# Gated tiles four ahead, the few tokens' rows in small pieces, weight units of both expert products in pairs of 1024 KB

## The chip, the cores and the metric

One core of a Trainium2 chip. The metric is the device time of one launch in microseconds. The kernel before takes 2781.53 us, the median of 3 runs (2779.76 to 2782.51).

## The reference

256 tokens of width 2048, everything in 32-bit floats, two blocks one after the other. The first has attention (16 forgetting heads, 16 dilated heads) and then a product-key expert layer, which is what the change is about:

```python
def peer(x, w_query, sub_keys, expert_down, expert_up):
    ...
    experts = (i1 * PEER_N_KEYS + i2).reshape(T, PEER_HEADS * PEER_TOPK)       # 128 of 16384 per token
    gates = jax.nn.softmax(top_vals, axis=-1).reshape(T, PEER_HEADS * PEER_TOPK).astype(x.dtype)
    ...
        u = jnp.take(expert_down, ec, axis=0)
        hdn = jax.nn.gelu(jnp.einsum('ted,td->te', u, xc))
        vsel = jnp.take(expert_up, ec, axis=0)
        return jnp.einsum('te,ted->td', gc * hdn, vsel)
```

The second block has a gated convolution, a chunked recurrence, an output product and a gated side input.

## The kernel before

**The expert layer is computed densely.** Instead of gathering 128 rows per token, the kernel multiplies 224 of the 256 tokens (`DENSE`) with all 16384 experts: the *down product* gives the hidden values of 128 experts per tile (`group_down`, 128 tiles), GELU is applied, each value is multiplied with its gate (zero for experts that weren't chosen; the gates are scattered into `gate_scratch` in HBM by 256 indirect DMAs of GpSimd and read back 8 tiles at a time by `load_g`), and the *up product* adds 128 gated tiles into eight PSUM banks. The last 32 tokens (`FEW`) are done the other way: GpSimd gathers 128 rows of 8 KB (1 MB) at a time, 32 times from `expert_down` and 32 times from `expert_up`, and VectorE multiplies and adds them (`few`, L1482 and L1487, one in about 1.4 tiles of the up product). What these tokens need (their expert numbers, gates, scale, their rows `x4` of the spilled activations, the gain row in `lent[0]`, the matrix `back`) is loaded by SyncE in the down product, at `FEW_LOADS`.

**Weights come as units** of [128, 1024] floats, 512 KB: two per tile in both products, 4 KB per partition. SyncE loads unit u into slot u % 4 of `raw` (`NRAW` = 4) when unit u - 4 has been split. ScalarE rounds it to whi (L1832, out whi, in raw), VectorE subtracts to get the remainder wlo (L1026), three units ahead of TensorE (`NSPL` = 3), and TensorE multiplies whi and wlo in turn (L590). Unit u may be split when TensorE has done unit u - 3. Each engine runs a list of steps that was written out by hand: `step(u)` ends with `split(u + 3)`, and whatever else an engine has to do stands before or behind it in a fixed order.

**A gated tile** of the up product is made by `weight(i)`: VectorE multiplies hidden values by gates (out HB, in HB and aX, L1029), ScalarE makes the rounded copy (L1832, out aX), VectorE subtracts (out aX, in HB and aX, L1029). For tile i + 2 this happens behind step 2i + 1 of the product, that is behind the split of the first unit of tile i + 2. TensorE waits for the gated tile (`s_ul`), for whi and for wlo. The copies stand in a ring of eight (`wring`).

**SyncE's list.** `now` = u - 6 while `load(u)` is the newest load. At `now == FEW_LOADS` 18 transfers are issued in a row. Gates are loaded every eighth tile (1 MB in rows of 1 KB), from the 64th tile on pieces of the spilled activations (256 KB). All are in the same queue as the weight units.

Of the kernel before, what the change touches and what calls it, by code (L numbers as in the profile page):

```python
# [147 lines left out]
def _build(nc, I, out, ctx):  # L148
# [135 lines left out]
    def lent_before(k):  # L284

        return [j for j in range(k) if lent_to(j) == lent_to(k)]

    FEW_AT = {(4 + 5 * k if k < 6 else 31 + 36 * (k - 6) // 25 if k < PICKS else 71 + 42 * (k - PICKS) // 31): k for k in range(2 * PICKS)}

    C = ExitStack()  # L290
# [32 lines left out]
    grow1 = HB[:, 8192:10240]  # L323
    C.close()

    plan = Plan(I)
    G = plan.groups
    for name, key in (("dv", "w_dv"), ("fv", "w_fv")):
# [34 lines left out]
    SCF = [plan.fill([b for b in range(4, 8) if b != R3F[0]][k % 3]) for k in range(8)]  # L363
    for i in range(128):
        plan.group("down", i, "w_down", i, 1, True)
    late = [G["down", 127].fills[0][0], G["down", 126].fills[0][0], R3F[0], SCF[-1][0]]
    early = [b for b in range(8) if b not in late]
    UPB = [early[0], early[1], late[0], late[1], early[2], early[3], late[2], late[3]]
# [2 lines left out]
    UPS = [(i, half) for i in range(120) for half in range(2)] + [(i, half) for half in range(2) for i in range(120, 128)]  # L371
    plan.src += [I["w_up"][i, :, half * UNIT:half * UNIT + UNIT] for i, half in UPS]
    UP1 = len(plan.src)
    for kp, b in enumerate((early[2], early[3], early[0], early[1], early[2], early[3], late[2], late[3])):
        plan.turn("mix", kp, plan.fill(b))
    plan.side_by_side("fl", "w_in2", range(40, 44), [plan.fill(b) for b in (early[0], early[1], late[0], late[1])])
# [30 lines left out]
    NU = len(plan.src)  # L407
    TURNED = plan.turned
    DOWN0 = G["down", 0].first
    FEW_LOADS = DOWN0 + 188  # L410
    down_rows, up_rows = I["down_rows"], I["w_up"].rearrange("i p d -> (i p) d")
    SQ0 = 6
    ROWS0 = G["dv", 1].first + 4
# [62 lines left out]
    def _(e):  # L476
        w = Gate(e)

        def load(u):
            if u >= NU:  # L480
                return
            if u >= NRAW:
                w.wait_ge(s_lo, u - NRAW + 1)
            e.dma_start(raw[:, u % NRAW, 0:plan.src[u].shape[-1]], plan.src[u]).then_inc(s_raw[u % NRAW], 16)

        def load_g(n, a=0, z=8):
            i = n % 2
# [8 lines left out]
        for u in range(NRAW, NU + NRAW + NSPL):  # L496
            load(u)
            if u == 6:
                e.dma_start(small[:, :], I["small"][:, 0:256]).then_inc(s_const, 16)
                e.dma_start(X[:, 0, :], I["x"][:, 0:D]).then_inc(s_x[0], 16)  # L500
            if u == 8:
                e.dma_start(X[:, 1, :], I["x"][:, D:2 * D]).then_inc(s_x[1], 16)
            if u == 11:
                e.dma_start(attc[:, :], I["att"]).then_inc(s_att, 16)
                e.dma_start(fbr[:, :], I["forget_bias"]).then_inc(s_att, 16)
            now = u - NRAW - NSPL + 1
            if now == G["fg", 0].end + 1:

                w.wait_ge(s_fc, 2)
                e.dma_start(c_d, cT[:, :]).then_inc(s_cd, 16)  # L510
                w.wait_ge(s_cd, 16)
                e.dma_start(CB[:, :, :].rearrange("p h c -> p (h c)"),
                            c_d.rearrange("h c -> (h c)").unsqueeze(0).to_broadcast([128, 4096])).then_inc(s_cb, 16)
            if now == PQ0 + 2:
                for i in range(2, 4):
                    for b, n in G["wf", i].fills:
                        w.wait_ge(s_free[b], n)
                e.dma_start(h1_d, X[:, :, :].rearrange("p t d -> p (t d)")).then_inc(s_spill, 16)
            if now == PQ0 + 5:

                for kp in range(8):
                    (b, n), q = TURNED["ffn", kp]
                    w.wait_ge(s_free[b], n)
                    w.wait_ge(s_nt, q + 1)
                w.wait_ge(s_spill, 16)
                e.dma_start(hb(5120, 2048), I["keys"]).then_inc(s_keys, 16)
            if now in ZERO:
                z = ZERO.index(now)
                w.wait_ge(s_zs, 1)
                e.dma_start(g_z[:, z * 2048:z * 2048 + 2048], zeros).then_inc(s_zf, 16)  # L530
            if now == FEW_LOADS:
# [6 lines left out]
                last = slice(128 - FEW, 128)  # L538
                for j in range(SHARE):
                    to, of = slice(FEW * j, FEW * j + FEW), slice(PICKS * j, PICKS * j + PICKS)  # L540
                    e.dma_start(eid4[to, :], eid[last, of]).then_inc(s_few, 16)
                    e.dma_start(gate4[to, :], gate[last, 1, of]).then_inc(s_few, 16)
                    e.dma_start(r4[to, :], st[last, 25:26]).then_inc(s_few, 16)
# [12 lines left out]
            if UP0 < now <= UP1 and (now - UP0) % 2 == 0:  # L556
                i = (now - UP0) // 2 - 1
                if i == 64:
                    w.wait_ge(s_uh, 66)
                    w.wait_ge(s_ul, 66)  # L560
                if i >= 64 and i % 4 == 0 and i < 96:
                    n = (i - 64) // 4
                    e.dma_start(HB[:, n * 512:n * 512 + 512], h1_d[:, n * 512:n * 512 + 512]).then_inc(s_h1r, 16)
                if i == 96:
                    e.dma_start(grow1, I["final_norm_gain"].to_broadcast([128, D])).then_inc(s_row1, 16)
            if now == G["fl", 0].first:

# [18 lines left out]
    def _(e):  # L586
# [125 lines left out]
        def tick(u):  # L712
# [11 lines left out]
            if u == ROWS3 + 4:  # L724
                row_of(R3F, 2, ones, diag)
            if u == UP1 - 16:
                w.wait_ge(s_few, 64 * SHARE + 32)
# [284 lines left out]
    def _(e):  # L1012
# [7 lines left out]

        def split(u):
            if u < NU:
                n, r, s = plan.src[u].shape[-1], u % NRAW, u % NSPL
                w.wait_ge(s_raw[r], 16 * (u // NRAW + 1))
# [567 lines left out]
        for i in range(120):  # L1592
# [4 lines left out]
                w.wait_ge(s_fg2, 1)  # L1597
                tt(hid4[:, :], hid4[:, :], gate4[:, :], ALU.mult).then_inc(s_fv, 1)
            step(UP0 + 2 * i + 1)
            weight(i + 2 + (i > 116))  # L1600
            if i == 116:
                weight(119)
            lower_bounds(i)
            if i == 90:
                tt(cols[:, C_NMX:C_NMX + 16], cols[:, C_NMX:C_NMX + 16], cols[:, C_FIN:C_FIN + 16], ALU.mult).then_inc(s_gm, 1)
        for j in range(16):
            step(UP0 + 240 + j)
            if j < 5:
                weight(123 + j)

        for j in range(2):
            for i in range(4):
# [129 lines left out]
    def _(e):  # L1742
# [39 lines left out]
        w.wait_ge(s_few, 64 * SHARE + 32)  # L1782
# [39 lines left out]
    def _(e):  # L1822
# [14 lines left out]

        def split(u):
            if u < NU:
                n, r, s = plan.src[u].shape[-1], u % NRAW, u % NSPL  # L1840
                w.wait_ge(s_raw[r], 16 * (u // NRAW + 1))
# [204 lines left out]
        for kt in range(16):  # L2046
            w.wait_ge(s_xt[XT_OF[kt]], 16)
            act(aX[:, kt, 0:256], xT[:, kt, :], ACT.Copy, scale=cols[:, C_ATT + kt:C_ATT + kt + 1]).then_inc(s_xh, 1)
            if kt in (1, 3):
                u = kt // 2  # L2050
                w.wait_ge(s_raw[u], 16)
                act(whi[:, u, 0:512], raw[:, u, 0:512], ACT.Copy).then_inc(s_h0, 1)
                act(whi[:, u, 512:1024], raw[:, u, 512:1024], ACT.Copy).then_inc(s_hi, 1)
            if kt in (7, 11):
                split((kt + 1) // 4)
        for name in ("dv", "fv"):
# [80 lines left out]
        for i in range(120):  # L2137
            step(UP0 + 2 * i)
            step(UP0 + 2 * i + 1)
            weight(i + 2 + (i > 116))  # L2140
            if i == 116:
                weight(119)
            if i == 68:
                w.wait_ge(s_fd2, PICKS)
                act(hid4[:, :], hid4[:, :], ACT.Gelu_apprx_tanh, scale=r4[:, 0:1]).then_inc(s_fg2, 1)
# [8 lines left out]
                warm()  # L2154
        for j in range(16):
            step(UP0 + 240 + j)
            if j < 5:
                weight(123 + j)

        for j in range(2):  # L2160
            for i in range(4):
# [104 lines left out]
def arrays(inp):  # L2266
# [11 lines left out]
    def toks(w):  # L2278
# [12 lines left out]
    a["w_out"] = toks(g["w_out"][0])  # L2291
    a["w_pq"] = feat(g["peer_query"][0])
    a["w_down"] = np.ascontiguousarray(
        g["peer_down"][0].reshape(128, 128, 2, 8, 128).transpose(0, 2, 4, 3, 1)).reshape(128, 2, 128, 1024)
# [34 lines left out]
```

## Time and profile before

| | |
|---|---|
| median of 3 runs | 2781.53 us (2779.76 to 2782.51) |
| the profiled execution | 2780.66 us, span of the core 2778.8 us |
| TensorE busy | 2731.4 us (98%) |
| VectorE, ScalarE, GpSimd busy | 1941.7, 1399.1, 794.8 us |
| mean granted clock of TensorE | 0.997 |
| moved by DMA | 628.32 MB, mean 226 GB/s |
| down product | about 496 to 1158 us |
| up product | about 1160 to 1895 us |

The span is one execution from its first to its last instruction; the time of that execution is 1.9 us longer. Engines work side by side, so busy shares don't add up to the span; what a wait costs is read from the engine that the others wait for. A line such as L1029 is that of a helper, so the tiles' names (out <- in) tell what an instruction does.

### The profile page before, as it was taken

To read this page: it belongs to the slowest core of one execution; us is meant where nothing else is said; L and a number is where in the kernel's file an instruction comes from. 1 tells how busy PE (TensorE), PEld (TensorE's weight loads), DVE (VectorE), ACT (ScalarE), POOL (GpSimd) and SP (SyncE) were. 2 spreads that over 40 slices of the span, in tenths; PEclk is the share of its full clock that TensorE was granted. 3 is DMA by queue.
4 is the path that set the end of the run, shared out by engine and by line. 5 is a ranking of instruction groups with operands and counts; after the bars stand their busy time and mean duration, and the time that the engine had idled before them with its cause. 6 is when DMAs were issued, how large, how long until landed. Compare 5 with 4: busy or idle time off the path is not lost.

```text
span 2778.8 us, 39198 instructions
## 1 busy us (share of the span) xinstructions
PE 2731.4 (98%) x14906; PEld 2369.9 (85%) x14906; DVE 1941.7 (70%) x2979; ACT 1399.1 (50%) x2003; POOL 794.8 (29%) x477
## 2 busy tenths in 40 slices
PE   9999999999999999999999999999999999999998
PEld 7887888999999989988777777778888888999886
DVE  6567666888888656666778788766778876555555
ACT  5455654555555545544444434446755545444454
POOL 0012200388888888400111121201201111000000
PEclk9999999999999999999999999999999999999999
DMA  7654478888888788777899999865655556666664
GB/s 275 209 166 134 147 254 301 277 209 209 210 209 209 209 212 208 235 249 267 314 335 326 323 339 352 321 219 185 190 179 153 162 157 193 189 189 188 187 199 157
DMA packets 205195, 628.32 MB, mean 226 GB/s; under 512 B 50944, under 2 KB 67600, under 8 KB 193616
## 3 DMA queue, kind: packets, MB, share of 16 engines
q1 hardware_dynamic: 162800, 558.24, 63.3%
q0 software_dynamic: 42064, 67.51, 8.8%
q8 instruction: 119, 1.95, 0.3%
q14 instruction: 68, 0.56, 0.1%
q10 hardware_dynamic: 144, 0.07, 0.0%
HBM read 604.59 MB, written 21.10 MB: 225 GB/s over the span
## 4 chain that ended last, share of the span: by engine, by line
PE 80%; DVE 8%; issue 4%; ACT 4%; DMA 3%; SPq 0%; DVEq 0%; POOL 0%; ACTq 0%
PE bank L590 80%; DVE wlo L1026 5%; ACT whi L1832 3%; DMA raw<-in_w_up 2%; PE bank L602 1%; DVE HB L1487 1%; DVE HB L1029 1%; DVE HB L1482 1%; DMA HB<-in_down_rows,eid 0%; ACT aX L1832 0%; DMA aX<-gate_scratch 0%; DMA raw<-in_w_down 0%; DMA VV<-in_xT 0%; ACT L1832 0%; DVE aX L1029 0%
## 5 line engine op out<-in xcount | busy, mean ns | idle before, releaser
L1026 DVE TENSOR_TENSOR wlo<-raw,whi 128x1024 fp32r<-128x1024 f32 (+1 forms) x965 | 1195.6, 1241 | 716.0 <-ACT whi L1832 712.1
L1832 ACT ACTIVATE whi<-raw 128x1024 fp32r<-128x1024 f32 (+1 forms) x967 | 1013.7, 1054 | 891.7 <-PE bank L590 840.1
L590 PE MATMUL bank<-whi,aX 128*128 128x512 f32 x2944 | 922.7, 392 | 25.5 <-DVE aX L1029 23.9
L590 PE MATMUL bank<-aX,whi 128*128 128x448 f32 (+2 forms) x4000 | 920.1, 379 | 0.0
L590 PEld LDWEIGHTS bank<-aX,whi 128*128 128x128 f32 (+1 forms) x4000 | 728.6, 188 | 98.7 <-issue 3.7
L590 PEld LDWEIGHTS bank<-whi,aX 128*128 128x128 f32 x2944 | 552.4, 188 | 159.9 <-DVE aX L1029 40.6
L590 PE MATMUL bank<-wlo,aX 128*128 128x512 f32 x1472 | 572.0, 390 | 1.4 <-DVE wlo L1026 1.4
L1777 POOL DMA_INDIRECT gate_scratch<-gate,place x256 | 529.3, 2067 | 77.9 <-issue 77.6
L590 PE MATMUL bank<-aX,wlo 128*128 128x224 f32 (+2 forms) x3984 | 513.5, 279 | 7.2 <-DVE wlo L1026 7.0
L590 PEld LDWEIGHTS bank<-aX,wlo 128*128 128x128 f32 (+1 forms) x3984 | 499.6, 191 | 22.8 <-DVE wlo L1026 8.0
L590 PEld LDWEIGHTS bank<-wlo,aX 128*128 128x128 f32 x1472 | 276.4, 188 | 58.4 <-DVE wlo L1026 2.5
L1832 ACT ACTIVATE aX<-HB 128x224 fp32r<-128x224 f32 x128 | 49.9, 391 | 316.6 <-DVE HB L1029 316.6
L1812 POOL TENSOR_TENSOR tmpc<-tmpc,rows 128x256 f32<-128x256 f32 x64 | 58.0, 906 | 405.8 <-DVE tmpc L1029 405.8
L1795 POOL DMA_INDIRECT HB<-in_down_rows,eid x32 | 50.7, 1586 | 335.7 <-DVE hid L1482 330.1
L1795 POOL DMA_INDIRECT HB<-in_w_up,eid x32 | 53.1, 1660 | 221.5 <-DVE HB L1487 177.5
L1750 POOL TENSOR_TENSOR EB<-EB,dn 128x256 f32<-128x256 f32 (+1 forms) x32 | 31.1, 992 | 276.6 <-DVE dn L1110 225.7
L1029 DVE TENSOR_TENSOR aX<-HB,aX 128x224 fp32r<-128x224 f32 x128 | 50.1, 392 | 57.6 <-ACT aX L1832 57.6
L1482 DVE CUSTOM_DVE_ANT_0 HB<-HB 128x2048 f32<-128x2048 f32 x32 | 73.1, 2284 | 0.7 <-DMA HB<-in_down_rows,eid 0.7
L1487 DVE SCALAR_TENSOR_TENSOR HB<-HB,hid 128x2048 f32<-128x2048 f32 x31 | 72.7, 2346 | 0.0
L1832 ACT ACT_TABLE_LOAD x52 | 66.7, 1283 | 2.5 <-PEq L2320 1.2
L1818 POOL TENSOR_TENSOR X<-X,grow 128x512 f32<-128x512 f32 x6 | 9.5, 1578 | 179.0 <-ACT scr L1832 179.0
L1029 DVE TENSOR_TENSOR HB<-bank,HB 128x224 f32<-128x224 f32 (+1 forms) x144 | 55.6, 386 | 3.7 <-ACT HB L1832 3.7
(246 smaller groups left out, 2066.6 us busy)
## 6 DMA issues: line engine op xcount, KB each, us to landing
raw<-in_w_down SPq DMA_DIRECT2D x256, 512.0 KB, 4.4
raw<-in_w_up SPq DMA_DIRECT2D x256, 512.0 KB, 5.4
raw<-in_w_in SPq DMA_DIRECT2D x176, 512.0 KB, 3.7
raw<-in_w_out SPq DMA_DIRECT2D x32, 512.0 KB, 4.2
gate_scratch<-HB SPq DMA_DIRECT2D x16, 1024.0 KB, 7.5
raw<-in_w_pq SPq DMA_DIRECT2D x32, 512.0 KB, 5.6
raw<-in_w_o SPq DMA_DIRECT2D x32, 512.0 KB, 4.1
raw<-in_w_pg SPq DMA_DIRECT2D x32, 512.0 KB, 3.7
```

What stands on the lines that cost most here:

```text
L590: return e.matmul(o, lhsT, rhs, start=start, stop=stop, skip_group_check=True)
L602: return e.transpose(o, src, ident)
L1026: e.tensor_tensor(wlo[:, s, 0:n], raw[:, r, 0:n], whi[:, s, 0:n].bitcast(F32), ALU.subtract).then_inc(s_lo, 1)
L1029: return e.tensor_tensor(o, a, b, op)
L1482: e.tensor_tensor_reduce(lent[n], lent[n], x4, 1.0, 0.0, ALU.mult, ALU.add, hid4[:, k:k + 1]).then_inc(s_fd2, 1)
L1487: e.scalar_tensor_tensor(acc4, lent[n], hid4[:, j:j + 1], acc4, ALU.mult, ALU.add).then_inc(s_fv, 1)
L1750: last = e.tensor_tensor(p, p, d2[:, :, k:k + 1].to_broadcast([128, 2, c.stop - c.start]), ALU.mult)
L1777: e.indirect_dma_start(g_d, bass.IndirectOffsetOnAxis(ap=place[0:some, t, n:n + 1], axis=0), gate[0:some, t, n:n + 1], None, compute_op=AL ...
L1795: e.indirect_dma_start(lent[n], None, up_rows if k >= PICKS else down_rows, bass.IndirectOffsetOnAxis(ap=eid4[:, k % PICKS:k % PICKS + 1], ...
L1812: e.tensor_tensor(h, h, rows4[:, :], ALU.mult).then_inc(s_rw, 1)
L1818: e.tensor_tensor(X2[:, t, f], X2[:, t, f], grow2[:, f], ALU.mult).then_inc(s_gg, 1)
L1832: return e.activation(o, i, f, **k)
```

## The change

Three things. **(1)** The up product's gated tiles are made up to four tiles ahead instead of two (`TILES_AT`; the lead is built up in the first six tiles, two of whose steps make two). **(2)** The transfers for the few tokens begin eight units earlier, at unit 180 of the down product; twelve small ones and `back` are issued in a row, the four pieces of `x4` (256 KB each) and the gain row in four pieces of 256 KB (rows of 2 KB) follow one by one, every third unit. **(3)** The two units of a tile of the down product, and of the first 120 tiles of the up product, are loaded by one transfer of 1024 KB into two neighbouring slots, 8 KB per partition (for that the down weights are laid out in HBM with both halves in a row). It is issued when unit u - 3 has been split, instead of u - 4, and both units wait for the same semaphore. `SLOT` shifts the slots by three so that pairs are neighbours.

```diff
+    TILES_AT, n = {}, 2
+    for i in range(120):
+        z = min(i + 3 + (i >= 2) + (i >= 5), 128)
+        TILES_AT[i] = range(n, z)
+        n = z
...
+    WIDE = {G["down", i].first: rows_down[i].rearrange("p (u c) -> p u c", u=2) for i in range(128)}
...
+    WIDE |= {UP0 + 2 * i: I["w_up"][i].rearrange("p (u c) -> p u c", u=2) for i in range(120)}
...
-    FEW_LOADS = DOWN0 + 188
+    SLOT = [(u + 3) % NRAW for u in range(NU)]
+    LANDED, landings = {}, [0] * NRAW
+    for u in range(NU):
+        if u - 1 in WIDE:
+            LANDED[u] = LANDED[u - 1]
+        else:
+            landings[SLOT[u]] += 16
+            LANDED[u] = s_raw[SLOT[u]], landings[SLOT[u]]
+    FEW_LOADS = DOWN0 + 180
+    X4_LOADS, GAIN_LOADS = [FEW_LOADS + 6 + 6 * j for j in range(SHARE)], [FEW_LOADS + 9 + 6 * j for j in range(4)]
...
         def load(u):
-            if u >= NU:
+            if u >= NU or u - 1 in WIDE:
+                return
+            r = SLOT[u]
+            if u in WIDE:
+                w.wait_ge(s_lo, u - NRAW + 2)
+                e.dma_start(raw[:, r:r + 2, :], WIDE[u]).then_inc(LANDED[u][0], 16)
                 return
             if u >= NRAW:
                 w.wait_ge(s_lo, u - NRAW + 1)
-            e.dma_start(raw[:, u % NRAW, 0:plan.src[u].shape[-1]], plan.src[u]).then_inc(s_raw[u % NRAW], 16)
+            e.dma_start(raw[:, r, 0:plan.src[u].shape[-1]], plan.src[u]).then_inc(LANDED[u][0], 16)
...
                     e.dma_start(r4[to, :], st[LAST, 25:26]).then_inc(s_few, 16)
-                    e.dma_start(x4[to, :], h1_d[last, D:2 * D]).then_inc(s_few, 16)
                 e.dma_start(back[:, :], I["small"][:, 256:384]).then_inc(s_few, 16)
-                e.dma_start(lent[0], I["ffn_norm_gain"].to_broadcast([128, D])).then_inc(s_few, 16)
+            if now in X4_LOADS:
+                j = X4_LOADS.index(now)
+                e.dma_start(x4[FEW * j:FEW * j + FEW, :], h1_d[LAST, D:2 * D]).then_inc(s_few, 16)
+            if now in GAIN_LOADS:
+                f = slice(GAIN_LOADS.index(now) * 512, GAIN_LOADS.index(now) * 512 + 512)
+                e.dma_start(lent[0][:, f], I["ffn_norm_gain"][:, f].to_broadcast([128, 512])).then_inc(s_few, 16)
...
             step(UP0 + 2 * i + 1)
-            weight(i + 2 + (i > 116))
-            if i == 116:
-                weight(119)
+            for x in TILES_AT[i]:
+                weight(x)
```

## Rows read from the trace of the kernel before

**Rows 1.** The page's first part: busy us, share, instructions of each engine.

```profile
PE 2731.4 (98%) x14906; PEld 2369.9 (85%) x14906; DVE 1941.7 (70%) x2979; ACT 1399.1 (50%) x2003; POOL 794.8 (29%) x477
```

**Rows 2.** Stretches: length, then busy PE, PEld, DVE, ACT, POOL; clock, DMA share, GB/s.

```profile
850.00:1000.00 150.00, 150.00 (x949) 142.29 (x949) 103.90 (x185) 81.60 (x123) 131.58 (x61) 1.00 0.80 207
1000.00:1020.00 20.00, 13.23 (x66) 12.22 (x65) 6.63 (x9) 5.47 (x9) 16.86 (x10) 0.74 0.91 261
1180.00:1350.00 170.00, 169.15 (x747) 139.72 (x746) 112.24 (x138) 74.46 (x93) 11.64 (x8) 1.00 0.76 262
1350.00:1830.00 480.00, 456.19 (x1959) 364.15 (x1958) 376.62 (x421) 199.41 (x255) 90.69 (x57) 1.00 0.92 331
```

**Rows 3.** Timeline of DVE, light part of the up product: start us, us, instruction, [idle before].

```profile
1244.61 1.22 DVE L1026 TENSOR_TENSOR wlo<-raw,whi 128x1024 fp32r<-128x1024 f32 x1 [1.21 <-ACT whi L1832]
...
1246.59 0.39 DVE L1029 TENSOR_TENSOR aX<-HB,aX 128x224 fp32r<-128x224 f32 x1 [0.46 <-ACT aX L1832]
1247.61 1.23 DVE L1026 TENSOR_TENSOR wlo<-raw,whi 128x1024 fp32r<-128x1024 f32 x1 [0.62 <-ACT whi L1832]
...
1252.03 0.39 DVE L1029 TENSOR_TENSOR aX<-HB,aX 128x224 fp32r<-128x224 f32 x1 [0.46 <-ACT aX L1832]
```

**Rows 4.** Waits in 1350 to 1830: who for whom, us in total, times, longest.

```profile
DVE wlo L1026 <- ACT whi L1832: 64.8, 85, 2.3
...
DVE aX L1029 <- ACT aX L1832: 37.5, 82, 0.5
...
PE bank L590 <- DVE aX L1029: 23.0, 36, 1.5
```

**Rows 5.** Timeline of DVE, crowded part: the subtractions that end three gated tiles.

```profile
1636.72 0.39 DVE L1029 TENSOR_TENSOR aX<-HB,aX 128x224 fp32r<-128x224 f32 x1 [0.46 <-ACT aX L1832]
...
1643.12 0.39 DVE L1029 TENSOR_TENSOR aX<-HB,aX 128x224 fp32r<-128x224 f32 x1 [0.46 <-ACT aX L1832]
...
1647.25 0.39 DVE L1029 TENSOR_TENSOR aX<-HB,aX 128x224 fp32r<-128x224 f32 x1 [0.46 <-ACT aX L1832]
```

**Rows 6.** Timeline of SyncE's queue and of ACT around the few tokens' transfers.

```profile
993.97 0.51 SPq L541 DMA_DIRECT2D eid<-eid  x1
...
995.79 0.58 SPq L544 DMA_DIRECT2D HB<-h_scratch  x1
...
1002.23 18.53 SPq L484 DMA_DIRECT2D raw<-in_w_down  x8
...
1010.43 1.06 ACT L1832 ACTIVATE whi<-raw 128x1024 fp32r<-128x1024 f32 x1 [10.20 <-DMA raw<-in_w_down]
```

**Rows 7.** Stretches of 2 us there, columns as in rows 2.

```profile
1006.00:1008.00 2.00, 0.10 (x1) 0.00 (x0) 0.00 (x0) 0.00 (x0) 1.69 (x2) 1.00 1.00 307
...
1012.00:1014.00 2.00, 1.14 (x5) 1.14 (x6) 2.00 (x3) 2.00 (x4) 1.95 (x1) 0.50 0.72 140
```

**Rows 8.** DMA issues, median us to landing: 520-990; 1180-1350 (two); 1350-1830 (two); 1250-1260.

```profile
raw<-in_w_down SPq DMA_DIRECT2D x186, 512.0 KB, 4.4
...
raw<-in_w_up SPq DMA_DIRECT2D x61, 512.0 KB, 4.7
...
HB<-in_down_rows,eid POOLq DMA_INDIRECT x8, 8.1
...
raw<-in_w_up SPq DMA_DIRECT2D x164, 512.0 KB, 5.9
...
HB<-in_w_up,eid POOLq DMA_INDIRECT x32, 8.7
...
raw<-in_w_up SPq DMA_DIRECT2D x3, 512.0 KB, 7.8
```

**Rows 9.** DMA issues of the whole run; then stretches, as rows 2, outside the products.

```profile
grow<-in_final_norm_g SPq DMA_DIRECT2D x1, 1024.0 KB, 5.8
...
2404.00:2406.50 2.50, 2.50 (x14) 2.09 (x14) 1.52 (x2) 1.52 (x3) 0.00 (x0) 1.00 0.68 210
...
2650.25:2653.50 3.25, 3.25 (x15) 2.65 (x15) 2.29 (x2) 2.22 (x3) 0.00 (x0) 1.00 1.03 416
```

More of the change, by code:

```diff
@@ L324, in _build @@
     C.close()
+    rows_down = I["w_down"]
+    I["w_down"] = rows_down.rearrange("i p (u c) -> i u p c", u=2)
     plan = Plan(I)
@@ L409, in _build @@
     DOWN0 = G["down", 0].first
-    FEW_LOADS = DOWN0 + 188
+    SLOT = [(u + 3) % NRAW for u in range(NU)]
[8 more added lines that the diff above has]
+    X4_LOADS, GAIN_LOADS = [FEW_LOADS + 6 + 6 * j for j in range(SHARE)], [FEW_LOADS + 9 + 6 * j for j in range(4)]
+    LAST = slice(128 - FEW, 128)
     down_rows, up_rows = I["down_rows"], I["w_up"].rearrange("i p d -> (i p) d")
@@ L537, in _ @@
                 w.wait_ge(s_spill, 16)
-                last = slice(128 - FEW, 128)
                 for j in range(SHARE):
                     to, of = slice(FEW * j, FEW * j + FEW), slice(PICKS * j, PICKS * j + PICKS)
-                    e.dma_start(eid4[to, :], eid[last, of]).then_inc(s_few, 16)
-                    e.dma_start(gate4[to, :], gate[last, 1, of]).then_inc(s_few, 16)
-                    e.dma_start(r4[to, :], st[last, 25:26]).then_inc(s_few, 16)
-                    e.dma_start(x4[to, :], h1_d[last, D:2 * D]).then_inc(s_few, 16)
+                    e.dma_start(eid4[to, :], eid[LAST, of]).then_inc(s_few, 16)
+                    e.dma_start(gate4[to, :], gate[LAST, 1, of]).then_inc(s_few, 16)
+                    e.dma_start(r4[to, :], st[LAST, 25:26]).then_inc(s_few, 16)
                 e.dma_start(back[:, :], I["small"][:, 256:384]).then_inc(s_few, 16)
-                e.dma_start(lent[0], I["ffn_norm_gain"].to_broadcast([128, D])).then_inc(s_few, 16)
+            if now in X4_LOADS:
[4 more added lines that the diff above has]
+                e.dma_start(lent[0][:, f], I["ffn_norm_gain"][:, f].to_broadcast([128, 512])).then_inc(s_few, 16)
             if now == UP0:
@@ L726, in tick @@
             if u == UP1 - 16:
-                w.wait_ge(s_few, 64 * SHARE + 32)
+                w.wait_ge(s_few, 64 * SHARE + 80)
                 w.wait_ge(s_fv, PICKS + 1)
@@ L1022, in split @@
             if u < NU:
-                n, r, s = plan.src[u].shape[-1], u % NRAW, u % NSPL
-                w.wait_ge(s_raw[r], 16 * (u // NRAW + 1))
+                n, r, s = plan.src[u].shape[-1], SLOT[u], u % NSPL
+                w.wait_ge(*LANDED[u])
                 w.wait_ge(s_hi, u + 1)
@@ L1607, in _ @@
             step(UP0 + 240 + j)
-            if j < 5:
-                weight(123 + j)
+            if j < 4:
+                weight(124 + j)
         for j in range(2):
@@ L1781, in _ @@
         e.dma_start(g0[:, :, :], g_v[:, 0:2, :]).then_inc(s_g0, 16)
-        w.wait_ge(s_few, 64 * SHARE + 32)
+        w.wait_ge(s_few, 64 * SHARE + 80)
         e.tensor_tensor(x4, x4, lent[0], ALU.mult).then_inc(s_fx, 1)
@@ L1839, in split @@
             if u < NU:
-                n, r, s = plan.src[u].shape[-1], u % NRAW, u % NSPL
-                w.wait_ge(s_raw[r], 16 * (u // NRAW + 1))
+                n, r, s = plan.src[u].shape[-1], SLOT[u], u % NSPL
+                w.wait_ge(*LANDED[u])
                 if u >= NSPL:
@@ L2050, in _ @@
                 u = kt // 2
-                w.wait_ge(s_raw[u], 16)
-                act(whi[:, u, 0:512], raw[:, u, 0:512], ACT.Copy).then_inc(s_h0, 1)
-                act(whi[:, u, 512:1024], raw[:, u, 512:1024], ACT.Copy).then_inc(s_hi, 1)
+                w.wait_ge(*LANDED[u])
+                act(whi[:, u, 0:512], raw[:, SLOT[u], 0:512], ACT.Copy).then_inc(s_h0, 1)
+                act(whi[:, u, 512:1024], raw[:, SLOT[u], 512:1024], ACT.Copy).then_inc(s_hi, 1)
             if kt in (7, 11):
@@ L2139, in _ @@
             step(UP0 + 2 * i + 1)
-            weight(i + 2 + (i > 116))
-            if i == 116:
-                weight(119)
+            for x in TILES_AT[i]:
+                weight(x)
             if i == 68:
@@ L2156, in _ @@
             step(UP0 + 240 + j)
-            if j < 5:
-                weight(123 + j)
+            if j < 4:
+                weight(124 + j)
         for j in range(2):
@@ L2293, in arrays @@
     a["w_down"] = np.ascontiguousarray(
-        g["peer_down"][0].reshape(128, 128, 2, 8, 128).transpose(0, 2, 4, 3, 1)).reshape(128, 2, 128, 1024)
+        g["peer_down"][0].reshape(128, 128, 2, 8, 128).transpose(0, 4, 2, 3, 1)).reshape(128, 128, 2048)
     a["down_rows"] = np.ascontiguousarray(g["peer_down"][0])
```

## Prediction

> **What bounds the kernel now.** The page first [rows 1]: TensorE is busy 2731.4 of 2778.8 us so at first sight nothing but TensorE counts. The stretches [rows 2] say where that is untrue: 6.8 us without a matmul in 1000 to 1020, at a mean clock of 0.74, and 23.8 us in 1350 to 1830; in 850 to 1000 nothing, in 1180 to 1350 0.9 us, both at full clock. The second stretch hides more than its idle time. Undisturbed, a tile of the up product (two weight units) takes 5.44 us from one gated tile to the next (1246.59 to 1252.03) [rows 3]; in 1350 to 1830 there are 82 gated tiles, at 5.44 us 446 us, and they took 480. So the loss there is 34 us.
>
> Who sets that pace? In 1350 to 1830 VectorE is busy 376.6 us and waits for ScalarE 64.8 + 37.5 us [rows 4]: sum 478.9 of 480, so VectorE never has to wait for TensorE. One tile in its order [rows 5]: remainder wlo of the even unit, gate times hidden (L1497's helper), wait 0.46 for ScalarE's rounded copy, subtraction, wait 0.62 for ScalarE's whi of the odd unit (queued behind that copy), remainder of the odd unit. From 1643.12 to 1647.25 that is 4.13 us; where a step of the few tokens' product (2.35 us) falls in, 1636.72 to 1643.12, 6.40 us. The two unavoidable waits are 1.08 x 82 = 88.6 us; busy plus these is 465.2, which is 19 us above TensorE's 446. The rest, 102.3 - 88.6 = 13.7 us, is late data: ScalarE splits late because its unit has not landed.
>
> The first stretch is one event [rows 6]. SyncE issues 18 transfers for the few tokens from 993.97 on and can issue the next unit's load only at 1002.23, 8.3 us later; that load shares the engines with 2 MB of rows and gains and lands at 1010.4, ScalarE having waited 10.20 us. TensorE is busy for 0.10 us of 1006 to 1008 and 1.14 us of 1012 to 1014, nothing between, and its clock, 1.00 as it stopped, is 0.50 (1.2 GHz of 2.4) when it resumes [rows 7]. By matmuls: 1000 to 1020 holds 66 where 850 to 1000 has 949 in 150 us [rows 2], that is 127 for 20 us; 61 x 0.158 us = 9.6 us.
>
> **The change part by part.** (1) *Small pieces.* SyncE now holds its queue for 13 issues: four groups of three and `back`. A group of three is 1.82 us (993.97 to 995.79) [rows 6], `back` about 0.5, so about 7.8 us, hardly less than before. But it begins right behind the load of a pair, and the next pair is due 5.02 us (a tile of the down product) later, so the delay is 2.8 us, and no 1 or 2 MB burst meets the load. The eight pieces of 256 KB follow every third unit (0.6 us of SyncE each, hidden). By the budget in (3) a pair may be some 2.5 us late before TensorE stands, so I leave 0.3 us and take 9.3 of the 9.6 us back; between 6 and 9.6.
>
> (2) *Tiles four ahead.* TensorE no longer waits for the gated tile (23.0 us of its waits in 1350 to 1830 end with VectorE's subtraction [rows 4]), but only for the remainder of its own unit, which VectorE finishes one um, copy and subtraction sooner: 1.2 us [rows 5]. VectorE's instructions, their order within a tile and both waits are the same, and it is VectorE that sets the pace in that stretch. So the 23.0 us are renamed, not removed: a once-only lead of 1.2 us. I take -1.2; between 0 and -5 (if it also smooths some of the late data).
>
> (3) *Pairs.* 512 loads of 512 KB become 248 of 1024 KB and 16 single ones. SyncE's issue time is no matter. What changes is how much lateness the loads may have. Before, unit u is requested when unit u-4 is split; now the pair (u, u+1) when u-3 is split, and the next-but-one request hangs on the split of u+1. That is a ring (the pairs of even and of odd number have one each, interleaved): request, landing L, whi 1.06 [rows 6], 0.1, wlo 1.22, then 3.0 us until the remainder of the odd unit is done (1245.83 to 1248.84 [rows 3]): L + 5.4 us for two tiles. TensorE's two tiles take 10.88 us, so the ring holds pace up to L = 5.45 us in the up product. Before, the ring was L + 2.4 for the same two tiles, with room to 8.4 us. In the down product the odd remainder follows the even one without the ScalarE round trip: L + 4.0 to 4.5 (one add, up to half a us of top-k work) for 10.04 us, so room to 5.6 to 6.0. Late by some 2.3 to 2.6 us once, TensorE isn't touched; late again and again, the ring sets the pace.
>
> What is L of a pair? No row has such a load. From below: a single load takes 4.4 us in the down product, 4.7 in the light part of the up product, 5.9 in the crowded part [rows 8]. A second 512 KB adds at least its bytes at the rate of the best stretch, 416 GB/s, 1.26 us [rows 9]; from the shape of a lone transfer (2.5 us at 210 GB/s, most of it ramp) about 1.0. From above: the only 1 MB load with 8 KB rows beside single loads there, `grow`, took 5.8 us behind a 512 KB one [rows 9]; and 2 x the 2.3 us a lone transfer lasts there gives +2.3. I take +1.1: down 5.5, light up 5.8. In the crowded part the engines are at 92% and 331 GB/s [rows 2]; there singles go from 4.7 to 5.9 while the 8 KB rows of the gathers only go from 8.1 to 8.7 [rows 8], so the long rows seem to get the larger share; with rows of 8 KB the pair should get a fairer one. I take 6.3 there (6.0 to 7.5).
>
> The Trainium skill (DMA: Bandwidth & Descriptors, Queues, rings and completion order) says that each engine goes round its queues packet by packet, which agrees with these landings; and the same page (Bandwidth) has the rule "Batch DMAs to ≥1 MiB for ≥75% of peak", which speaks for the pairs. By that page's fit for GpSimd's queue, 2.0 us + bytes/436e3, an estimate for 1 MB is 4.4 us, inside the room of 5.45, and the pairs would cost nothing.
>
> Price, up product. Light part, 30 tiles: (5.8 + 5.4) - 10.88 = 0.3 per two tiles, 5 us; each of four gate loads (1 MB ahead in the same queue; singles around the one at 1251.7 take 7.8 us [rows 8]) adds about 1 us that nothing gives back: 7 to 9, I take 8. Crowded part, 82 tiles: ring 6.3 + 5.4 = 11.7 against the 480/41 = 11.7 that it takes now: equal, but the ten gate loads now have no room: 1 to 1.5 us each, I take 12. Behind it nothing (no gathers, half the traffic). Down product: 5.5 against 5.6 to 6.0, 1 us for everything (0 to 8). Sum of pairs +21; from 0 (L = 4.4 to 5.0) to +55 (L one us longer: 0.5 us x 112 tiles more). Below zero too: with fairer shares the 13.7 us of late data may go.
>
> **Sum.** Profiled execution: 2780.66 us, of which the span is 2778.8. -9.3 - 1.2 + 21 = +10.5: 2791. The median of the runs is 0.9 us above the profiled one: I say 2792.
>
> **The rivals.** *A, pairs land in time* (faster). L of a pair is 5.0 or less. Then the ring costs nothing, the hiccup's 9.3 us and the 1.2 are won and some of the 13.7: 2781.5 - 10.5 - 8 = 2763. For it: rate 416 GB/s once a transfer runs, and that engines at 59% leave gaps; against it: 4.7 us for a single even in the light part. (The Trainium skill's batching rule, cited above, would give this case.) *A2, the idle time goes*: the tiles ahead remove the 23.8 us as the waits name them: 2781.5 - 9.3 - 24 = 2748. Against it: VectorE's full 478.9 us. *B, it balances*: pairs cost 5 to 14 us and the hiccup's return pays for it: 2781 ± 5. *C, the ring everywhere* (slower by more): L is 7 us or above in the crowded part and 6.5 in the down product; from L = 6.0 on the down product pays too, 256 units / 4 x 0.5 = 32 us, the up product 35 to 45: 2830.
>
> **Chances.** Forecast (2787 to 2810) 0.42; B 0.20; A 0.24; A2 0.05; C 0.09. A measurement of this kernel tells about 0.2%, 5.6 us, from no change: faster 0.29, same 0.20, slower 0.51. Signs are mixed, so beside the likeliest case's own 2787 to 2810 the range reaches from A's middle to the gap before C: 2760 to 2816.
>
> **What the profile after would show.** Landing of the 1024 KB loads: 5.5 / 5.8 / 6.3 us in the down, light and crowded parts; at 5.0 the forecast is wrong on the fast side. 1000 to 1020 with full clock and at most 1 us idle. TensorE's waits for the gated tile gone, and in their place waits for wlo; in 1180 to 1350 new idle of 5 to 10 us where there is 0.9 now. ScalarE's waits for the DMA of w_up stand at even units only, and are 40 us or more in all. VectorE's tile still 4.13 and 6.40 us where data is there. The forecast is wrong if the crowded part takes under 478 us, or if the down product's matmuls per us stay at 6.33 and the light part's at 4.39, for then the ring never closes.

## The result, and the profile after

The changed kernel takes 2803.43 us (median of 4 runs, 2801.33 to 2805.46), the kernel before, beside it, 2780.65 us (2778.54 to 2782.51): ratio 1.008, 95% interval 1.0065 to 1.0095. It is slower by 22.8 us. 2792 was forecast, range 2760 to 2816, slower with a chance of 0.51. The profiled execution is the slowest of the four (2805.46 us); its span is 2803.7 us, 24.9 more than before, and what is read from the two traces below adds up to that.

First the stretches of the changed kernel, columns as in [rows 2]:

```profile
1000.00:1020.00 20.00, 20.00 (x128) 18.97 (x128) 12.65 (x17) 11.56 (x20) 16.90 (x11) 1.00 0.93 265
...
1160.00:1180.00 20.00, 16.50 (x82) 13.64 (x80) 8.42 (x13) 8.68 (x14) 0.00 (x0) 0.97 0.61 212
1180.00:1350.00 170.00, 166.39 (x713) 134.40 (x714) 108.11 (x137) 71.97 (x92) 10.36 (x7) 0.98 0.69 244
1350.00:1850.00 500.00, 471.73 (x1970) 360.75 (x1969) 380.00 (x421) 199.94 (x255) 87.15 (x57) 1.00 0.87 320
```

The hole at 1000 us is gone: 128 matmuls at full clock where [rows 2] had 66. Against that, 1180 to 1350 holds 713 matmuls (747 before) with 3.6 us without a matmul (0.9 before), and the crowded part makes 1970 in 500 us, 3.94 per us; [rows 2] has 1959 in 480, 4.08. Two milestones divide the 24.9 us. VectorE's last scaling of a down tile (out HB, in HB and bank) starts 5.2 us sooner than before:

```profile
1173.34 0.39 DVE L1029 TENSOR_TENSOR HB<-HB,bank 128x224 f32<-128x224 f32 x1
```

in the timeline of VectorE before, and after

```profile
1168.16 0.39 DVE L1056 TENSOR_TENSOR HB<-HB,bank 128x224 f32<-128x224 f32 x1
```

TensorE's first transpose behind the up product comes 24.5 us later:

```profile
1894.97 0.60 PE L602 MATMUL bank<-small,X 128*128 128x128 f32 x4
```

in the timeline of TensorE before, and after

```profile
1919.44 0.60 PE L629 MATMUL bank<-small,X 128*128 128x128 f32 x4
```

So the up product took 29.7 us more, all before it 5.2 us less, and what lies behind it 0.4 us more (24.9 - 24.5).

Inside the up product the loss is placed by VectorE's timelines, by the start of the remainder (wlo) of the same unit in both traces (us; units of the up product counted from 0):

| unit | before | changed | changed later by |
|---|---|---|---|
| 0 | 1166.74 | 1161.55 | -5.2 |
| 8 | 1190.20 | 1190.45 | 0.3 |
| 64 | 1342.53 | 1348.71 | 6.2 |
| 240 | 1857.56 | 1882.04 | 24.5 |

The border of the two products cost 5.4 us, the light part 5.9, the crowded part 18.3, together the same 29.7. Now the waits of the changed kernel's whole run (who for whom: us in total, times, longest):

```profile
ACT whi L1858 <- DMA raw<-in_w_up: 134.1, 70, 5.3
ACT whi L1858 <- DMA raw<-in_w_down: 117.7, 56, 5.2
...
PE bank L617 <- DVE wlo L1053: 35.1, 58, 2.0
```

Before, the first two were 24.9 us (20 times) and 13.7 us (4 times). ScalarE now waits for nearly every second pair. TensorE's waits no longer name the gated tile (23.0 us in [rows 4]) but the remainder wlo. The 117.7 us in the down product hardly reach TensorE (2976 matmuls in 520 to 990, 2981 before), those in the up product do.

**The ring, seen once without and once with a gate load.** Timelines of VectorE, SyncE's queue and ScalarE in the changed kernel's light part, put in order of time (start us, us, instruction, [idle before]):

```profile
1211.14 1.23 DVE L1053 TENSOR_TENSOR wlo<-raw,whi 128x1024 fp32r<-128x1024 f32 x1 [0.56 <-ACT whi L1858]
...
1212.39 0.33 SPq L504 DMA_DIRECT2D raw<-in_w_up  x1
1212.77 0.43 SPq L514 DMA_DIRECT2D aX<-gate_scratch  x1
...
1216.83 0.33 SPq L504 DMA_DIRECT2D raw<-in_w_up  x1
...
1217.32 1.06 ACT L1858 ACTIVATE whi<-raw 128x1024 fp32r<-128x1024 f32 x1 [1.77 <-DMA raw<-in_w_up]
...
1218.48 1.23 DVE L1053 TENSOR_TENSOR wlo<-raw,whi 128x1024 fp32r<-128x1024 f32 x1 [1.68 <-ACT whi L1858]
...
1221.41 1.23 DVE L1053 TENSOR_TENSOR wlo<-raw,whi 128x1024 fp32r<-128x1024 f32 x1 [0.56 <-ACT whi L1858]
...
1224.04 1.06 ACT L1858 ACTIVATE whi<-raw 128x1024 fp32r<-128x1024 f32 x1 [2.66 <-DMA raw<-in_w_up]
```

An odd unit's remainder ends at 1212.37; SyncE requests the pair after the next at 1212.39; it lands at 1217.3, 4.9 us later; the even remainder follows at 1218.48 and the odd one ends at 1222.64. The ring was 10.27 us long, L + 5.4 as forecast, and under the 10.88 us of two tiles. The next pair was requested at 1216.83, behind the gate load of 1212.77, and took 7.2 us: its ring is 7.2 + 5.4 = 12.6, 1.7 us too long. (The page has no landing time for the 1024 KB loads; landings here are from SyncE's issue to the start of ScalarE's split where that waited for the transfer.) A landing can be read in this way only where ScalarE waited, so the early ones are missing. In the down product the mean of 56 such pairs was 5.5 us: the first six, beside the zeroing of the gate scratch, took 6.6 to 8.3 us, the 50 others 4.8 to 6.8, half of them at most 5.2. In the light part three pairs behind a gate load took 6.8 to 7.9 us and 14 others 4.7 to 7.3, nine of them at most 5.0. In the crowded part the mean of 51 pairs was 6.3 us, and 7.1 for the eleven of those just behind a gate load.

**The border of the two products**, which the forecast had not looked at. SyncE's queue and VectorE in the changed kernel:

```profile
1172.72 0.33 SPq L504 DMA_DIRECT2D raw<-in_w_up  x1
1173.17 0.97 SPq L514 DMA_DIRECT2D aX<-gate_scratch  x2
...
1180.10 0.39 DVE L1056 TENSOR_TENSOR HB<-HB,aX 128x224 f32<-128x224 f32 x1 [6.03 <-DMA aX<-gate_scratch]
```

and SyncE's queue before:

```profile
1173.04 0.33 SPq L484 DMA_DIRECT2D raw<-in_w_up  x1
1173.49 0.97 SPq L490 DMA_DIRECT2D aX<-gate_scratch  x2
```

The first gate loads are issued at the same moment in both, though the changed kernel was 5.2 us ahead. In SyncE's list they stand behind a weight load; as a pair it waits for one split more. VectorE stood 6.03 us for the gates; before it was 2.51:

```profile
1181.90 0.39 DVE L1029 TENSOR_TENSOR HB<-HB,aX 128x224 f32<-128x224 f32 x1 [2.51 <-DMA aX<-gate_scratch]
```

The stretch 1160 to 1180 holds 82 matmuls instead of 106.

### The profile page after: what moved, and what is told of

It reads as the page before. It is cut to its first block, busy times and chain, and to the rows that moved or that the text cites. A ratio compares the mean times of both kernels' runs of the same rounds, so it can differ in the third digit from the quotient of the medians.

```text
span 2803.7 us, 38457 instructions
## 1 busy us (share of the span) xinstructions
PE 2748.5 (98%) x14906; PEld 2361.8 (84%) x14906; DVE 1943.4 (69%) x2979; ACT 1398.0 (50%) x2003; POOL 753.6 (27%) x477
## 4 chain that ended last, share of the span: by engine, by line
PE 72%; DVE 11%; DMA 8%; ACT 6%; issue 3%; DVEq 0%; POOL 0%; SPq 0%; ACTq 0%
PE bank L617 71%; DMA raw<-in_w_up 7%; DVE wlo L1053 7%; ACT whi L1858 5%; DVE HB L1509 1%; DVE HB L1514 1%; DVE HB L1056 1%; PE bank L629 1%; DMA raw<-in_w_down 1%; ACT aX L1858 0%; ACT L1858 0%; DMA raw<-in_w_dv 0%; DMA aX<-gate_scratch 0%; DVE QKb L1056 0%; DVE aX L1524 0%
## 5 line engine op out<-in xcount | busy, mean ns | idle before, releaser
L617 PE MATMUL bank<-whi,aX 128*128 128x512 f32 x2944 | 940.7, 395 | 37.2 <-DVE wlo L1053 31.1
L1803 POOL DMA_INDIRECT gate_scratch<-gate,place x256 | 492.9, 1925 | 77.9 <-issue 77.7
```

What stands on the lines that cost most here:

```text
L617: return e.matmul(o, lhsT, rhs, start=start, stop=stop, skip_group_check=True)
L1803: e.indirect_dma_start(g_d, bass.IndirectOffsetOnAxis(ap=place[0:some, t, n:n + 1], axis=0), gate[0:some, t, n:n + 1], None, compute_op=AL ...
```

## The experiments

Two theories at first. *Ring*: requesting pairs late closes a ring through transfer, ScalarE and VectorE, and costs in the up product; in the crowded part VectorE's own chain sets the pace in both kernels. *Rival*: not the time of the request but the transfer's size, or the tiles made ahead, or the traffic as such. Intervals are 95%, ratios to the kernel before on the same chip. All edits are to the changed kernel unless told otherwise, and kernel 1 is that of experiment 1, and so on. A profiled execution can lie some us off its kernel's median, so traces tell where time goes and medians how much.

**1. Without pairs (no_pairs).**

```diff
-    WIDE = {G["down", i].first: rows_down[i].rearrange("p (u c) -> p u c", u=2) for i in range(128)}
+    WIDE = {}
...
-    WIDE |= {UP0 + 2 * i: I["w_up"][i].rearrange("p (u c) -> p u c", u=2) for i in range(120)}
```

(the down weights lie in HBM as before)

> The changed kernel with single loads of 512 KB everywhere; tiles four ahead and small pieces stay. Ring theory (the pairs are the loss, the late request closes a ring through ScalarE and VectorE): 2781 less 9.6 for the hole at 1000 us and less 1 to 5 for the tiles ahead, 2766 to 2771. Rival (the pairs are innocent and making tiles four ahead costs the time): stays near 2800.

Measured: 2770.23 us, ratio 0.996 (0.9946 to 0.9974). The pairs are the whole loss, 33 us, and the rest of the change is a gain of 10.6 us.

**2. Late single loads (late_singles).**

```diff
         def load(u):
-            if u >= NU or u - 1 in WIDE:
+            if u >= NU:
                 return
             r = SLOT[u]
             if u in WIDE:
                 w.wait_ge(s_lo, u - NRAW + 2)
-                e.dma_start(raw[:, r:r + 2, :], WIDE[u]).then_inc(LANDED[u][0], 16)
-                return
-            if u >= NRAW:
+            elif u >= NRAW:
                 w.wait_ge(s_lo, u - NRAW + 1)
```

> The changed kernel, but each pair is loaded as two transfers of 512 KB with rows of 4 KB, both issued at the moment at which the pair was, each with its own semaphore. Ring theory: the even unit lands earlier by the second half's transfer, about 0.5 to 1 us (3.9 to 4.4 instead of 4.9), so part of the loss remains: 2785 to 2795. Rival (it is the 1 MB transfer itself, its size and rows, that disturbs others): 2766 to 2772, as without pairs. Rival (rows of 8 KB are what saves the pair among the gathers): slower than 2803.

Measured: 2812.5 us, ratio 1.011 (1.0093 to 1.0127): 42 us slower than kernel 1, whose transfers have the same size and are requested sooner (its down weights lie in HBM as before, here with both halves in a row), and 9 us slower than the pairs (1.0065 to 1.0095; the intervals just touch). It is the time of the request, not the transfer's size, that costs; one long transfer in place of two short ones is rather a gain. I had expected the even half to land early enough to win something; the third expectation came true. Its crowded part has 1872 matmuls in 480 us (the changed kernel 1893 in the same stretch):

```profile
1340.00:1820.00 480.00, 453.08 (x1872) 346.97 (x1872) 357.94 (x404) 189.57 (x241) 87.40 (x54) 0.99 0.90 317
```

(columns as in [rows 2]). Two short transfers differ from a pair in row length and in their number; which of the two helps was not tried apart.

**3. Pairs in the down product alone (pairs_down).**

```diff
-    WIDE |= {UP0 + 2 * i: I["w_up"][i].rearrange("p (u c) -> p u c", u=2) for i in range(120)}
```

> Pairs in the down product alone, singles in the up product. Ring theory: landings of 4.9 to 5.4 us are inside the down product's room of 5.6 to 6.0 us, so only the first ten tiles (landings of 6.6 to 8.3 us beside the zeroing of the gate scratch) and the border cost: 1 to 5 us above the kernel without pairs, 2769 to 2774. Rival (pairs cost the same per unit anywhere): half of the loss, 2785.

Measured: 2772.55 us, ratio 0.997 (0.9958 to 0.9981), 2.3 us above the kernel without pairs, within what the intervals can tell. The same transfers cost little in the down product, where the ring has no trip through ScalarE, and some 31 us in the up product, where it has. The up product also has more traffic; kernel 5 tells the two apart.

**4. Gates first, without pairs (gates_first).** From kernel 1. VectorE multiplies by the gates before the split and subtracts behind it; ScalarE's list is untouched.

```diff
-            step(UP0 + 2 * i + 1)
             for x in TILES_AT[i]:
-                weight(x)
+                gate_tile(x)
+            step(UP0 + 2 * i + 1)
+            for x in TILES_AT[i]:
+                low_tile(x)
```

(`gate_tile` and `low_tile` are the two halves of VectorE's `weight`)

> Without pairs, and VectorE multiplies a tile's hidden values by its gates before the split of the even unit instead of behind it, and subtracts behind it; ScalarE's order stays. Its two waits per tile (0.46 and 0.6 us) should lie behind the split. Theory that VectorE's chain of 4.13 and 6.40 us per tile sets the crowded part: the chain falls to about 3.1 and 5.4 us, below TensorE's 5.44, and the 34 us lost in 1350 to 1830 go but for late data: 2738 to 2750. Rival (the crowded part is held by the transfers, at 331 GB/s near their limit): within 8 us of the kernel without pairs.

Measured: 2760.43 us, ratio 0.9918 (0.9901 to 0.9935): 10 us less than kernel 1, not 20 to 30. The chain did shorten. VectorE's timeline of this kernel, a tile with a step of the few tokens:

```profile
1599.66 0.38 DVE L1053 TENSOR_TENSOR aX<-HB,aX 128x224 fp32r<-128x224 f32 x1
1600.09 1.22 DVE L1050 TENSOR_TENSOR wlo<-raw,whi 128x1024 fp32r<-128x1024 f32 x1
1601.23 2.35 DVE L1518 SCALAR_TENSOR_TENSOR HB<-HB,hid 128x2048 f32<-128x2048 f32 x1
1603.50 0.38 DVE L1053 TENSOR_TENSOR HB<-HB,aX 128x224 f32<-128x224 f32 x1
1603.80 1.22 DVE L1050 TENSOR_TENSOR wlo<-raw,whi 128x1024 fp32r<-128x1024 f32 x1
1604.93 0.38 DVE L1053 TENSOR_TENSOR aX<-HB,aX 128x224 fp32r<-128x224 f32 x1
...
1609.54 1.23 DVE L1050 TENSOR_TENSOR wlo<-raw,whi 128x1024 fp32r<-128x1024 f32 x1 [2.66 <-ACT whi L1864]
```

From subtraction to subtraction 5.27 us instead of 6.40 [rows 5], no wait inside. But then comes one of 2.66 us, and it is for data. The waits in 1340 to 1820 of kernel 1,

```profile
ACT whi L1855 <- DMA raw<-in_w_up: 29.8, 21, 2.9
```

and of this kernel:

```profile
ACT whi L1864 <- DMA raw<-in_w_up: 110.1, 59, 5.9
```

So both theories were right in part: the chain held the crowded part, and behind it, 10 us further, stood the transfers. The second half rests on these waits, and on kernel 11 below, where gathers at a lower rate gave more.

**5. Gates first, with all pairs (gates_first_pairs).** The same edit on the changed kernel.

> The changed kernel, all pairs kept, with VectorE's multiplication by the gates ahead of the split of the even unit and its subtraction behind it. The way from the even to the odd remainder loses its trip through ScalarE (3.0 us become about 1.6), so the ring is L + 4.0 and has room to 6.9 us instead of 5.45. Ring theory: most of the up product's loss goes, 10 to 25 us less than the changed kernel's 2803 beyond what the same reordering gives without pairs (10 us): 2768 to 2783. Rival (pairs cost because four slots hold too little in any order): 2793, the reordering's 10 us alone.

Measured: 2765.15 us, ratio 0.9937 (0.992 to 0.9954), 38 us less than the changed kernel where the same edit gave 10 without pairs. Nothing in the transfers was changed; only the way from the even to the odd remainder was shortened. The expectation for the ring was 2768 to 2783; the gain was larger than that, 28 us beyond the reordering's own against 10 to 25. This is the strongest evidence for the ring. Nor did the pairs land sooner: read as above, the mean in 1350 to 1850 was 7.1 us (71 pairs), 6.3 in the changed kernel. ScalarE waits even longer for data than in the changed kernel, and TensorE far less:

```profile
ACT whi L1867 <- DMA raw<-in_w_up: 209.1, 73, 5.8
...
PE bank L617 <- DVE wlo L1053: 14.6, 17, 2.1
```

in 1340 to 1820; the changed kernel, in 1350 to 1850:

```profile
ACT whi L1858 <- DMA raw<-in_w_up: 96.9, 52, 5.3
...
PE bank L617 <- DVE wlo L1053: 28.2, 48, 2.0
```

**6. Tiles two ahead (no_ahead).**

```diff
-        z = min(i + 3 + (i >= 2) + (i >= 5), 128)
-        TILES_AT[i] = range(n, z)
-        n = z
+    TILES_AT = {i: [i + 2 + (i > 116)] + [119] * (i == 116) for i in range(120)}
```

> The changed kernel with tiles two ahead as before; pairs and pieces stay. My step: the lead is worth about 1.2 us once, so 2802 to 2808. Rival (the lead is what lets late pairs through, for a late unit then no longer holds a tile): 2815 or more. Rival (making tiles ahead costs): under 2800.

Measured: 2798.71 us, ratio 1.0066 (1.0046 to 1.0085), 4.7 us less than the changed kernel, where 2802 to 2808 had been expected; the third expectation (making tiles ahead costs) named this time. But the intervals (1.0065 to 1.0095 against 1.0046 to 1.0085) overlap, so that the lead costs anything beside pairs is not shown. The traces put the difference in the light part: from unit 8 to unit 64 this kernel falls back 1.0 us against the kernel before (1189.27 to 1342.63), the changed one 5.9. The ring, L + 5.4, is the same in both, and doesn't explain that; the cause was not tried.

**7. Small pieces alone (pieces_only).** Kernel 1 with tiles two ahead, that is the kernel before with the new loads for the few tokens.

> The kernel before with the small pieces for the few tokens alone. The hole at 1000 us was put at 9.6 us: 2771 to 2774. If it is 2770 like the kernel without pairs, the tiles ahead are worth nothing; if 2776 or more, the hole's clock loss was overrated and the tiles ahead give the rest.

Measured: 2772.94 us, ratio 0.9968 (0.9957 to 0.998): -8.7 us, against 9.3 in the forecast. Kernel 1, with the lead, is 2.7 us lower, or 2.0 lower when each is taken against the kernel before beside it; that too is within the intervals.

**8. Gate loads ahead of the pair at the border (border).**

```diff
         for u in range(NRAW, NU + NRAW + NSPL):
+            if u == UP0 + NRAW + NSPL - 1:
+                w.wait_ge(s_mm, UP0)
+                for t in range(2):
+                    w.wait_ge(s_gs[t], 2048)
+                load_g(0, 2, 8)
+                load_g(1)
             load(u)
...
-            if now == UP0:
-                w.wait_ge(s_mm, UP0)
-                for t in range(2):
-                    w.wait_ge(s_gs[t], 2048)
-                load_g(0, 2, 8)
-                load_g(1)
```

> The changed kernel with the up product's first two gate loads issued ahead of the pair for units 6 and 7 of that product instead of behind it. After the change they were issued at 1173.2, though the down product was over some 5 us sooner, and VectorE waited 6.0 us for them. If the border is a term of its own: 4 to 6 us less than 2803, about 2798. If the pair that now stands behind the gates takes it back: 2801 to 2806.

Measured: 2795.11 us, ratio 1.0046 (1.0027 to 1.0064): -8.3 us, more than the 4 to 6 expected. SyncE's queue in this kernel:

```profile
1163.79 0.97 SPq L514 DMA_DIRECT2D aX<-gate_scratch  x2
```

9.4 us sooner than in the changed kernel. So the border is a term of its own. Its size in the change is the 5.4 us between units 0 and 8: in this kernel unit 8 starts at 1182.33, 7.9 us sooner than in the kernel before, and VectorE no longer waits for the gates at all, so the edit also takes back the 2.5 us that it waited there before the change.

**9. Both (gf_pairs_border).** Kernel 5 with the edit of 8.

> The changed kernel with the multiplication by the gates ahead of the split and the first gate loads ahead of the pair, both together. If the two terms are separate they add: 2765 less 4 to 8 is 2757 to 2761. If the border's gain came only from a ring that had no room, it shrinks now: 2762 to 2766.

Measured: 2760.58 us, ratio 0.9912 (0.9895 to 0.993), 4.6 us less than kernel 5, inside the 2757 to 2761 of two terms that add. The intervals of kernels 5 and 9 overlap, so whether the border's term is as large here as in kernel 8 is open.

**10 to 12. The few tokens' steps spread out.** All three also have the edits of 4 and 8.

```diff
-        return 0 if k < 6 else (k + 1) % 2 if k < 12 else (14 - k) % 3
+        return 0 if k < 9 else k % 2 if k < 13 else (15 - k) % 3
...
-    FEW_AT = {(4 + 5 * k if k < 6 else 31 + 36 * (k - 6) // 25 if k < PICKS else 71 + 42 * (k - PICKS) // 31): k for k in range(2 * PICKS)}
+    FEW_AT = {(4 + 3 * k if k < 9 else 30 + 36 * (k - 9) // 22 if k < PICKS else 71 + 46 * (k - PICKS) // 31): k for k in range(2 * PICKS)}
```

With all pairs (gf_pairs_spread):

> As gf_pairs_border, and the few tokens' 64 steps are spread over the up product: nine in tiles 4 to 28 instead of six, then one per 1.64 tiles instead of 1.44, and one per 1.5 instead of 1.35 in the second half, so the gathers ask for less per us. With the gates first, what is left of the crowded part's loss should be late transfers at 337 to 339 GB/s. If so: 5 to 15 us less than gf_pairs_border, 2745 to 2755. Rival (late data comes from bursts and gate loads, not from the mean rate): within 3 us of it.

Measured: 2756.82 us, ratio 0.9903 (0.9886 to 0.9919), only 3.8 us less than kernel 9; 5 to 15 were expected, within 3 by the rival, so this one speaks rather for the rival. With single loads (gf_spread):

> Single loads of 512 KB, gates first, first gate loads ahead of the load that stood before them, few tokens spread. From 2760: the border is worth 0 to 2 here (a single load holds SyncE for less long), spreading 5 to 15: 2744 to 2755.

Measured: 2749.58 us, ratio 0.988 (0.9863 to 0.9897), as expected, and 10.9 us less than kernel 4 (which lacks the edit of 8). Why spreading gives more without pairs than with them was not tried. With pairs in the up product alone (gf_up_spread):

> As gf_pairs_spread, but with pairs in the up product alone. In the crowded part the reordered kernel with pairs had more matmuls than the one without (2020 against 2004 in 480 us), while down product and border had fewer. Ring theory: now that the ring of the up product has room, pairs with long rows help there and singles are better in the down product: the fastest of the four, 2742 to 2752. Rival (long rows give nothing): as gf_spread.

Measured: 2753.22 us, ratio 0.9896 (0.9879 to 0.9912). It had been expected to be the fastest of the four, and isn't: even with a ring that has room, no gain of pairs over single loads shows. The intervals of kernels 11 and 12 overlap, and in 1340 to 1820 kernel 12 made 2067 matmuls and kernel 11 2055, so a small gain there and a loss elsewhere aren't ruled out. The lowest median, kernel 11's, is without pairs. It is 32.5 us below the kernel before, and its crowded part (columns as in [rows 2]) makes 2055 matmuls in the 480 us in which kernel 1 makes 1963:

```profile
1340.00:1820.00 480.00, 470.24 (x2055) 383.90 (x2054) 374.86 (x430) 215.01 (x266) 89.83 (x53) 1.00 0.91 333
```

## Why the prediction was right, and where it was off

| term | forecast, us | measured, us | by |
|---|---|---|---|
| small pieces | -9.3 (6 to 9.6) | -8.7 | kernel 7 |
| tiles four ahead | -1.2 (-5 to 0) | -2.0 without pairs, +4.7 with; neither clear of noise | kernels 1 and 7; 6 |
| pairs, down product | +1 (0 to 8) | +2.3 | kernels 3 and 1 |
| pairs, up product | +20 | +31 | changed kernel and 3 |
| sum | +10.5 | +22.8 | |

The rows add up with the lead as it is without pairs; what it does beside pairs is in the last row.

The mechanism of the forecast came true: late requests close a ring in the up product, and its cost outweighs the two gains. Its size was half of what was measured, 10.5 against 22.8 us, and the range of 2760 to 2816 reached over faster and slower kernels alike, so that the time fell inside says less than the terms do.

*What bounds the kernel.* That VectorE's chain and not TensorE or the transfers set the crowded part was read from busy 376.6 + waits 102.3 = 478.9 of 480 us. Kernel 4 bears it out, for a reordering that removes no instruction gave 10 us. What the reading could not show was how close the next bound stood: I expected 20 to 30 us of that edit.

*Small pieces.* Right in place and size. 1000 to 1020 is full, at full clock; the pair behind the 13 issues came late (ScalarE waited up to 5.2 us for w_down) and TensorE did not notice, as the 2.8 us of delay in the forecast would have it.

*Tiles ahead.* That the 23.0 us would be renamed, not removed, is what happened: they are now waits for wlo. The size was taken from a single lead; beside pairs the median moved the other way, within the noise.

*Pairs.* The mechanism was right, and its constants were: ring L + 5.4, 10.27 us with L = 4.9; VectorE's tile is 4.07 and 6.28 us in the light part (4.13 and 6.40 forecast from the crowded one), as the timeline of the changed kernel's subtractions shows:

```profile
1227.19 0.39 DVE L1056 TENSOR_TENSOR aX<-HB,aX 128x224 fp32r<-128x224 f32 x1 [0.46 <-ACT aX L1858]
...
1233.47 0.39 DVE L1056 TENSOR_TENSOR aX<-HB,aX 128x224 fp32r<-128x224 f32 x1 [0.46 <-ACT aX L1858]
...
1237.54 0.39 DVE L1056 TENSOR_TENSOR aX<-HB,aX 128x224 fp32r<-128x224 f32 x1 [0.46 <-ACT aX L1858]
```

The term that was mis-sized is the up product's 20 us. In the light part I had L = 5.8 at all times; it was about 4.9 where nothing stood in the way and 7.2 behind a gate load, so the ring had room between gate loads, and its price there was 5.9 us instead of 8 (642 matmuls in 1200 to 1350, 664 before, which is 5.0 us). In the crowded part L was 6.3, as I had it; but the price was 18.3 us by the units (17 by the matmuls: 1970 where 4.08 per us would have made 2040), and I had 12. The step that failed there is the comparison of means: a ring of mean 11.7 us against a mean pace of 11.7 is not free, for landings went from 4.8 to 8.6 us, and a pair that is late can't be made good by one that is early. That this spread is the whole of the missing 6 us is argued, not shown. A whole term was missing: the border, 5.4 us. To ask of every load that is moved what stands behind it in its queue would have found it: a pair that waits for one split more holds everything that stands behind it in SyncE's list, and the first gate loads stand there. The three together are the 29.7 us of the milestones; the medians of the changed kernel and kernel 3 give 31.

*The signs.* As forecast, ScalarE's waits for w_up were over 40 us (134.1) and the crowded part did not get shorter. The down product kept its 6.33 matmuls per us (2976 in 470 us) while the light part fell from 4.39 to 4.19 (713 in 170 us); the sign against the ring asked for both to stay. New idle time in 1180 to 1350 was put at 5 to 10 us and was 3.6, but 34 matmuls fewer are 7.7 us at 4.39 per us, so idle time alone told too little. One sign misled: "at 5.0 the forecast is wrong on the fast side". Undisturbed pairs landed in 4.9, and the kernel was slower.

*The rivals.* A ("pairs land in time", L of 5.0 or less) is instructive, for L was 4.9 where nothing stood in the way, in both products, and yet its outcome did not come. The condition was put on the undisturbed landing; what counted were the disturbed ones, one in eight behind a gate load and 37 of the 51 that ScalarE waited for in the crowded part, which took over the 5.45 us that the ring has room for. The Trainium skill (DMA: Bandwidth & Descriptors, Bandwidth) has the rule to batch to 1 MiB; as a rule on transfers the trace agrees (4.9 us for 1 MB beside 4.4 to 4.7 for 512 KB, and kernel 2 is 9 us slower than the pairs). What decided here was another thing, how late the large load could be requested. A2 is refuted by the waits for wlo; C did not come, since the down product paid only 2.3 us. Two of the prediction's sums don't come out: 0.5 us x 112 tiles on top of 21 is +77 and not +55, and C's terms add up to 2838 to 2848 and not 2830. The forecast uses neither, but the price of a landing one us longer was understated.

## What to carry to other kernels

Before loads are merged, write down the ring: from the moment a slot is free, through request, landing and every step until it is free again, and compare it with the time TensorE needs for what the slots hold, with the landing as it is behind the worst neighbour in the same queue and not undisturbed. The way from the first half of a merged load to the second (here 3.0 us, with a trip through another engine in it) counts in full, and shortening it (kernel 5) was worth 38 us, 10 of which it gives without pairs too; the merging had cost 33. And when a load waits longer, look at what stands behind it in its queue.

## What the runs showed of the hardware

Undisturbed, the 1 MB of a pair landed in 4.7 to 5.0 us in the light part; read in the same way, the quickest even units of kernel 2, 512 KB requested at the same point, took 4.0 to 4.2 (1227.9, 1239.5 and 1336.4 us). So the second half cost about 0.7 us, less than the 1.1 that I took from the rate of 416 GB/s. Kernels 11 and 12 have landings of both sizes in the list of DMA issues, and there the double size did not show: the median is 5.2 us for 512 KB and 5.1 for 1024 KB in 1180 to 1350, 6.9 and 6.3 in 1340 to 1820 (a single load can have its neighbour before it in the queue; the two weren't taken apart).

And the gathers did not lose to the long rows: their 1 MB lands in 6.5 us in the crowded part of the changed kernel (median; 8.7 before; all queues together moved 320 GB/s instead of 331), so the fairer share that the forecast gave the pairs was not seen; in kernel 1, without pairs, it was 9.4 us. At nearly equal traffic, in 1340 to 1820, the gathers of w_up took 8.2 us in kernel 5 (pairs, 339 GB/s) and 9.6 in kernel 4 (single loads, 337 GB/s). Why was not tried.
